# Layer-norm statistics partly on ScalarE, and the first two slabs of each up projection in buffers of their own

## The reference

```
for i in range(DEPTH):                                   # DEPTH = 2
    mix = _gmlp_mixer(h, ...) if i % 2 == 0 else _rwkv7_mixer(h, ...)
    h = _layer_norm(ALPHA * h + mix, ln1_g[i], ln1_b[i], LN_EPS)
    f = jnp.square(jax.nn.relu(h @ ffn_w1[i])) @ ffn_w2[i]
    h = _layer_norm(ALPHA * h + f, ln2_g[i], ln2_b[i], LN_EPS)

def _layer_norm(x, g, b, eps):
    mean = jnp.mean(x, axis=-1, keepdims=True)
    var = jnp.mean(jnp.square(x - mean), axis=-1, keepdims=True)
    return (x - mean) * lax.rsqrt(var + eps) * g + b
```

## Time and profile before

| | us |
|---|---|
| median of 3 runs | 1327.91 |
| lowest and highest | 1326.28, 1327.91 |
| the profiled execution's own time | 1330.27 |
| its span in the trace | 1328.6 |
| its mean granted TensorE clock | 0.988 of full speed |

### The profile page before, as it was taken

One profiled execution on the slowest core, in us unless ns is written; L12 is line 12 of the kernel. 1 busy time (PEld: TensorE's weight loads), 2 busy tenths in 40 slices (PEclk: granted clock), 3 DMA queues, 4 the chain that ended last, 5 costly groups with the idle time before them and its releaser, 6 DMA issues.

```text
span 1328.6 us, 22895 instructions
## 1 busy us (share of the span) xinstructions
PE 1282.6 (97%) x9137; PEld 1058.8 (80%) x9137; DVE 681.6 (51%) x922; ACT 497.3 (37%) x842; POOL 572.4 (43%) x353
## 2 busy tenths in 40 slices
PE   6999999999999998999999999999999999999996
PEld 5888788888888885487777888888798888888885
DVE  2486831112244468844478888876751111344447
ACT  4363232223223323234444667667222222322230
POOL 4344344444444452145454456644054444444440
PEclk9999999999999998999999999889999999999998
DMA  8234253332453331275443112112353333333321
GB/s 285 69 95 123 62 143 96 95 95 79 145 141 112 108 95 48 85 255 183 142 159 113 35 50 82 34 50 81 95 146 100 101 97 95 95 95 95 96 62 64
DMA packets 113579, 139.53 MB, mean 105 GB/s; under 512 B 10416, under 2 KB 86240, under 8 KB 113504
## 3 DMA queue, kind: packets, MB, share of 16 engines
q1 hardware_dynamic: 108896, 121.67, 30.5%
q10 hardware_dynamic: 4608, 16.78, 3.4%
HBM read 123.76 MB, written 14.68 MB: 104 GB/s over the span
## 4 chain that ended last, share of the span: by engine, by line
PE 76%; DVE 16%; ACT 4%; issue 2%; DMA 1%; SPq 1%; ACTq 0%; DVEq 0%
PE bank L1731 36%; PE bank L1826 9%; PE bank L1828 9%; PE bank L1827 9%; DVE a_lo L1181 2%; DVE gram L1539 2%; DVE x_tok L1211 2%; DVE x_tok L1213 2%; DVE stats L1200 2%; PE bank L1921 2%; DVE x_tok L1233 1%; PE bank L2038 1%; PE bank L2086 1%; PE bank L2204 1%; DMA raw<-in_gm_w_in 1%
## 5 line engine op out<-in xcount | busy, mean ns | idle before, releaser
L489 POOL TENSOR_TENSOR w_lo<-raw,w_hi 128x1024 fp32r<-128x1024 f32 x176 | 432.6, 2463 | 608.5 <-ACT w_hi L683 558.4
L683 ACT ACTIVATE w_hi<-raw 128x1024 fp32r<-128x1024 f32 x176 | 184.3, 1056 | 280.9 <-PE bank L1731 268.7
L1731 PE MATMUL bank<-w_hi,a_hi 128*128 128x512 f32 x756 | 234.8, 392 | 5.9 <-DVE a_lo L1181 5.9
L1826 PE MATMUL bank<-xT_hi,w_hi 128*128 128x512 f32 (+1 forms) x640 | 236.3, 369 | 3.9 <-POOL w_lo L489 3.9
L1827 PE MATMUL bank<-xT_lo,w_hi 128*128 128x512 f32 (+1 forms) x640 | 235.4, 368 | 0.0
L1828 PE MATMUL bank<-xT_hi,w_lo 128*128 128x512 f32 (+1 forms) x640 | 235.4, 368 | 0.0
L1731 PE MATMUL bank<-w_lo,a_hi 128*128 128x512 f32 x756 | 233.0, 389 | 0.0
L1731 PE MATMUL bank<-w_hi,a_lo 128*128 128x512 f32 x756 | 232.9, 389 | 0.0
L1181 DVE TENSOR_TENSOR a_lo<-big,a_hi 128x512 fp32r<-128x512 f32 x64 | 141.3, 2213 | 178.5 <-ACT a_hi L702 175.4
L1298 DVE TENSOR_TENSOR big<-relu 128x512 f32 (+1 forms) x64 | 45.8, 716 | 274.1 <-ACT relu L808 274.1
L1731 PEld LDWEIGHTS bank<-w_hi,a_hi 128*128 128x128 f32 x756 | 140.1, 188 | 40.4 <-issue 12.3
(11 more groups left out here) (310 smaller groups left out, 1639.6 us busy)
## 6 DMA issues: line engine op xcount, KB each, us to landing
raw<-in_ffn_w SPq DMA_DIRECT2D x128, 512.0 KB, 3.9
raw<-in_rw_w_rkv SPq DMA_DIRECT2D x24, 512.0 KB, 3.6
raw<-in_gm_w_in SPq DMA_DIRECT2D x16, 512.0 KB, 4.1
early<-proj SPq DMA_DIRECT2D x8, 1024.0 KB, 6.5
proj<-stage ACTq DMA_DIRECT2D x14, 512.0 KB, 3.6
proj<-low_stage ACTq DMA_DIRECT2D x10, 512.0 KB, 5.0
raw<-in_gm_w_out SPq DMA_DIRECT2D x8, 512.0 KB, 3.6
late<-proj SPq DMA_DIRECT2D x8, 512.0 KB, 4.1
```

Of the source, the lines that this page charges most:

```text
L489: nc.gpsimd.tensor_tensor(w_lo[:, j, :], raw[:, j, :], w_hi[:, j, :].bitcast(F32), ALU.subtract).then_inc(w_lo_ready, 1)
L683: nc.scalar.activation(w_hi[:, j, :], raw[:, j, :], ACT.Copy).then_inc(w_hi_ready, 1)
L1731: last = nc.tensor.matmul(bank[2 * t + h][:], a[:, j, tok], w[:, h * HALF:(h + 1) * HALF], start=start and m == 0, stop=stop and m == 2)
L1826: nc.tensor.matmul(dst, w_hi[:, j, col], xT_hi[:, k, tokens], start=k == 0, stop=False)
```

## The change

**Statistics.** For tiles 0 to 2 of each norm, `add` now also sums its output (`accum_out`). DVE forms the negative mean from the two sums (`less_mean`). ACT squares the whole tile with that as bias into a scrap buffer, with a sum (`square_sum`), and takes the root of it with scale 1/1024 and epsilon as bias (`deviation_of`). Tile 3 keeps `bn_stats`.

**Order on DVE.** The two passes over tile t - 1 now stand between the two `add`s of tile t, and for tile 2 further apart. `low_x` of tile 0 stands ahead of tile 3's first `add`, `low_x` of tile 1 behind its `bn_stats`.

**Own buffers.** The first two slabs of `up0` and `up1` are rounded into `first_hi` and their rest goes to `first_lo`, both in space of `big` that is idle then. So they wait for no slot of the row product; for `up1` they wait for the last readers of what lay there. Behind them ACT issues a root of epsilon, which loads the root's table.

```diff
+            def low_up(layer):
+                i = first_slab[f"up{layer}"] // SLOTS
+                for j in range(FIRST):
+                    pool.wait_ge(w_hi_ready, i * SLOTS + j + 1)
+                    nc.gpsimd.tensor_tensor(first_lo[:, j, :], raw[:, j, :], first_hi[:, j, :].bitcast(F32), ALU.subtract
+                                            ).then_inc(w_lo_ready, 1)
+                for j in range(FIRST, SLOTS):
+                    low_weights(i, j)
...
+            def deviation_of(norm, t):
+                count = (norm - 1) * (TT - 1) + t + 1
+                act.wait_ge(mean_ready, count)
+                nc.scalar.activation(junk[:], x_tok[:, t, :], ACT.Square, bias=less_mean[:, 0:1],
+                                     accum_out=square_sum[:]).then_inc(squares_summed, 1)
+                act.wait_ge(squares_summed, count)
+                nc.scalar.activation(std[:], square_sum[:], ACT.Sqrt, bias=eps[:, 0:1], scale=1.0 / D
+                                     ).then_inc(std_ready, 1)
...
             def finish_norm(name, count, norm, times, rounded=False):
+                if rounded:
+                    for j in range(FIRST):
+                        act.wait_ge(raw_in[j], 16 * ((first_slab[name] + count) // SLOTS + 1))
+                        if name == "rw_out":
+                            act.wait_ge(a_lo_ready, first_act[name] + KT)
+                            act.wait_ge(slab_used, first_slab[name] + SLOTS)
+                        nc.scalar.activation(first_hi[:, j, :], raw[:, j, :], ACT.Copy).then_inc(w_hi_ready, 1)
+                    nc.scalar.activation(std[:], eps[:], ACT.Sqrt)
+                deviation_of(norm, 0)
+                deviation_of(norm, 1)
+                if times is not None:
+                    turned(times, 0, rounded)
+                deviation_of(norm, 2)
+                if times is not None:
+                    turned(times, 1, rounded)
+                if rounded:
+                    for j in range(FIRST, SLOTS):
+                        round_weights(count // SLOTS, j, first_slab[name])
+                std_of(TT + norm)
...
+                for t in range(TT - 1):
+                    then(add(t, 0))
+                    if t:
+                        reciprocal_of(t - 1)
+                        centre(t - 1, whole, less_mean[:, 0:1], ALU.add)
+                        scaled(t - 1, whole).then_inc(x_ready, 1)
+                    then(add(t, 1))
+                    nc.vector.tensor_scalar(less_mean[:], y_sums[:, t % 2, 0:1], y_sums[:, t % 2, 1:2], -1.0 / D, ALU.add, ALU.mult
+                                            ).then_inc(mean_ready, 1)
...
+                def own(f):
+                    return (first_hi[:, f, :], first_lo[:, f, :]) if f < FIRST else None
                 for f in range(SLOTS):
-                    column_slab(0, f, n0, slice(0, 2 * P), False)
+                    column_slab(0, f, n0, slice(0, 2 * P), False, own(f))
```

More of the change, by code:

```diff
@@ L733, in turned, with std_of @@
                                          ).then_inc(xT_ready, 1)
-            def std_of(norm, t):
-                act.wait_ge(var_ready, norm * TT + t + 1)
+            def std_of(count):
+                act.wait_ge(var_ready, count)
                 nc.scalar.activation(std[:], mean_var[:, 1:2], ACT.Sqrt).then_inc(std_ready, 1)
-            def finish_norm(name, count, norm, times, rounded=False):
[L741 to L752, removed]
-                if times is not None:
-                    for t in range(2 if rounded else TT - 1, TT):
+            def deviation_of(norm, t):
[6 more added lines that the diff above has]
+                                     ).then_inc(std_ready, 1)
@@ L778, in _ @@
                 if f in (1, 2, 3, 4):
[L779 removed]
+                    std_of(f)
                 ahead(f // SLOTS, f % SLOTS, n0)
@@ L1204, in normalise @@
                                         ).then_inc(var_ready, 1)
-                if between is not None:
-                    between()
                 dve.wait_ge(std_ready, var_before + 1)
[L1208 to L1214, removed]
+                then(nc.vector.reciprocal(rstd[:, 0:1], std[:]))
+                then(nc.vector.scalar_tensor_tensor(y, y, mean_var[:, 0:1], gains[:, 0, :], ALU.subtract, ALU.mult))
+                nc.vector.scalar_tensor_tensor(y, y, rstd[:, 0:1], gains[:, 1, :], ALU.mult, ALU.add).then_inc(result, 1)
             def residual_norm(name, which, times, split=True):
@@ L1220, in residual_norm, with add @@
                 product = row_products.index(name)
[L1221 to L1229, removed]
-                        else:
[L1231 to L1240, removed]
+                def add(t, h):
+                    if h == 0:
+                        if t == 0:
+                            dve.wait_ge(tile_summed, product * (TT - 1) + 1)
+                        else:
+                            dve.wait_ge(half_summed, normed.index(name) * (TT - 1) + t)
+                    elif t < TT - 1:
+                        dve.wait_ge(tile_summed, product * (TT - 1) + t + 1)
+                    else:
+                        dve.wait_ge(slab_used, first_slab[name] + COUNT[name])
+                    y = x_tok[:, t, h * HALF:(h + 1) * HALF]
+                    return nc.vector.scalar_tensor_tensor(y, y, ALPHA, bank[2 * t + h][:], ALU.mult, ALU.add,
+                                                          accum_out=y_sums[:, t % 2, h:h + 1])
@@ new lines, in centre, with scaled, reciprocal_of @@
+                def centre(t, part, mean, op):
+                    y = x_tok[:, t, part]
+                    then(nc.vector.scalar_tensor_tensor(y, y, mean, gains[:, 0, part], op, ALU.mult))
+                def scaled(t, part):
+                    y = x_tok[:, t, part]
+                    return nc.vector.scalar_tensor_tensor(y, y, rstd[:, t % 2:t % 2 + 1], gains[:, 1, part], ALU.mult, ALU.add)
+                def reciprocal_of(t):
+                    dve.wait_ge(std_ready, (which + 1) * TT + t + 1)
+                    then(nc.vector.reciprocal(rstd[:, t % 2:t % 2 + 1], std[:]))
@@ new lines, in residual_norm @@
+                last = TT - 1
+                if times is not None and split:
+                    low_x(0, times)
+                then(add(last, 0))
+                done.inc(nc.vector.bn_stats(stats[:, 0, :], x_tok[:, last, parts[0]]))
+                if times is not None and split:
+                    low_x(1, times)
+                reciprocal_of(last - 1)
+                centre(last - 1, whole, less_mean[:, 0:1], ALU.add)
+                then(add(last, 1))
+                then(nc.vector.bn_stats(stats[:, 1, :], x_tok[:, last, parts[1]]))
@@ new lines, in residual_norm @@
+                then(nc.vector.bn_aggr(mean_var[:], stats[:].rearrange("p h s -> p (h s)")))
+                nc.vector.tensor_scalar(mean_var[:, 1:2], mean_var[:, 1:2], LN_EPS, None, ALU.add
+                                        ).then_inc(var_ready, 1)
+                scaled(last - 1, whole).then_inc(x_ready, 1)
+                reciprocal_of(last)
+                for part, ready in zip(parts, (x_half, x_ready)):
+                    centre(last, part, mean_var[:, 0:1], ALU.subtract)
+                    scaled(last, part).then_inc(ready, 1)
@@ L1268, in _ @@
                 split_x(t, 0)
+            then(nc.vector.memset(eps[:], LN_EPS))
             dve.wait_ge(gains_in, 32)
```

35 lines of the change are left out of this document (24 added, 11 removed).

## The result

The changed kernel took **1316.92 us** (median of 4 runs, 1316.32 to 1317.34), the kernel before 1327.5 beside it (4 runs): ratio 0.9921, 95% interval 0.9904 to 0.9939, 10.6 us faster. Both intervals leave out 1. The profiled execution took 1316.32 us, its span is 1314.5 and its granted clock 0.996.

What follows compares the result with a forecast made beforehand. TensorE, busy 97% of the span, bounds the kernel, so only its waits around the norms can pay: 2 x 3.1 (norms 1, 3) + 2 x 0.6 (norms 2, 4) = 7.4 us, from 1327.91 to 1320.5 us, range 1318.0 to 1325.5.

Steps and rivals of the forecast that it cites:

- Norm 4 is the same chain: Norm 4's tail behind TensorE's last matmul was taken to be like norm 2's, gaining 0.6 us.
- Up projections: First passes of up0 and up1: 3.44 us of stalls each, of which 3.1 us would be gained in each.
- The 0.3 us kept for `xT_lo`: First slab of an up projection: 0.3 of its 1.71 us wait remains, for xT_lo of tiles 0 and 1.
- the third stall: First pass of up0, turning of tile 3: TensorE waits 1.33 us, which the change would remove.
- Tiles 0 and 1, no gain: Statistics of tiles 0 and 1: x_ready comes where it was, since the saved instructions become waiting for TensorE; gain nothing.
- The sums: Writing out a sum with an add on DVE costs 0.1 us, and the same on ACT.
- Rival B: The sums are dear, at 0.7 us each: 6.0 us slower, 1333.9; decides from about 0.5 a sum; chance 0.07.
- the 0.5 us that ACT was to have to spare: Tile 0's root: ACT's sum hides behind TensorE's half tile with 0.5 us to spare, the root ready at about 142.8.
- The root's table, 0: Ahead of norm 1's first root: the 1.28 us table load is already finished early, so loading ahead is worth 0.
- Rival A: POOL starts ahead of DVE's pass over tile 2, margin 0.3 us: costs 1.3 us per up projection, time 1323.1; chance 0.17.
- Rival C: The stalls only move to the turnings, norms 2 and 4 give nothing: 2.8 us or less, 1325.1 and above; chance 0.11.
- The clock: Behind norm 2, TensorE's granted clock may shift the time by 1.5 us either way, in every case.

Runs made afterwards that it cites:

- s3_norm4_old: The changed kernel with the old code for norm 4 alone; 1319.73 us, norm 4 at 25.06.
- a1_after: The changed kernel again, nothing edited, on another chip; 1318.17 us, ratio 0.9935 to the kernel before.
- s1_buffers: The kernel before plus only the own buffers for the first two slabs of both up projections; 1324.97 us against 1326.74, ratio 0.9981.
- s2_stats: The changed kernel without the own buffers, so new order and statistics alone; 1323.34 us against 1326.74 for the kernel before, ratio 0.9975.
- s7_order_only: The changed kernel with bn_stats back on VectorE, no sums, ACT squares or root ahead; 1324.46 us against 1326.64 for the kernel before, ratio 0.9977.
- s4_no_root_ahead: The changed kernel without the root of epsilon that loads the root's table ahead; 1319.78 us.
- s5_pass_late: The changed kernel with tile 2's first pass behind the last add and its bn_stats in norms 1 and 3; 1322.81 us, ratio 0.9979 to the kernel before.

## Why the prediction was too low, step by step

**The step that failed** is "Norm 4 is the same chain" and the 0.6 us taken from it. Norm 2's tail behind PE was 7.03 us; norm 4's was 8.84, and I had not read it. After the change both have about the same tail, 6.31 in norm 4 and 518.11 - 511.83 = 6.28 in norm 2, since DVE no longer falls behind. PE's and DVE's timeline at the end of norm 2 after, for the earlier trace rows:

```profile
511.44 0.39 PE L1807 MATMUL bank<-w_hi,a_lo 128*128 128x512 f32 x1
```
```profile
517.36 0.75 DVE L1272 SCALAR_TENSOR_TENSOR x_tok<-x_tok,rstd,gains 128x512 f32<-128x512 f32 x1
```

Norm 2 gained 0.76, where 0.6 was forecast; norm 4 gained 2.55. s3_norm4_old shows it. With 2.55 in its place the same sum is 3.1 + 3.1 + 0.6 + 2.55 = 9.35, 1318.6. With all four as measured it is 10.3, and 1327.5 - 10.3 = 1317.2 is within 0.3 of the result. That the time came out at 1316.92 and not a little over 1318, as a1_after's 1318.17 did, goes with the granted clock (0.995 to 0.996 against mostly 0.993); that norm 4's gain was sized at a quarter does not depend on it.

**Up projections**: right mechanism, 3.5 in place of 3.1 each: all of the 3.44 us of stalls went. The 0.3 us kept for `xT_lo` came to nothing visible: the first slab's weight load has a wait of 0.39 in its row, but its first matmul starts right behind the product's last (157.70 + 0.39 = 158.09). s1_buffers and s2_stats show that the two parts need each other for the third stall.

**Tiles 0 and 1, no gain**: right against the kernel before, but s7_order_only shows that ACT's statistics are what holds this at nothing; without them norms 1 to 3 are 1.1 to 1.4 us longer each than in the changed kernel. The prediction costed the parts only together.

**The sums** (0.1 each): DVE's extra instruction takes 0.08 but lies in the end of the add: from an add to the next dependent instruction it is 0.72 us before (1301.05 to 1301.77) and 0.73 with the sum (159.42 to 160.15). ACT's takes 0.18. Rival B, which needed 0.5, is out. But the 0.5 us that ACT was to have to spare were 0.1 (143.31 to 143.43): the square, its sum and the root took until 143.31, not 142.8.

**The root's table, 0**: right in net. Its load is 1.28 us in the rows, and s4_no_root_ahead has 1.05 us of it on the path.
The Trainium skill ("ScalarE: Activation LUTs", section "What ACT_TABLE_LOAD costs") gives about 2.66 us for a change of table, 1.28 for the load and 1.38 for a drain. The trace agrees with the load, and a drain of that length does not show: in s4_no_root_ahead the load starts 0.01 us behind the square's sum and the root 0.02 behind the load.

**Rival A** did not come (158.10 against 158.64, so 0.5 us of margin, not 0.3), and s5_pass_late shows that it was a real one, 1.7 us each. **Rival C** is out: no stall moved.

**The clock**: I gave it 1.5 us behind norm 2 alone. Between two profiles of one kernel it made 3.75 us, most of it in the time mixing. So medians on two chips say 10.6 and 8.5 for a change whose columns give 10.3 us, and s1_buffers (1.8 measured, 4.6 in its columns) and s7_order_only (2.2 measured, 5.2 in its columns) look small. That the clock makes all of this is inferred from the middle column and the windows. In s1_buffers' runs, 1321.52 us goes with 0.993 and 1328.56 with 0.986. Why some versions are granted less clock than others stays open.

## What to carry to other kernels

Read the tail behind the last matmul at each place where a pattern recurs, and compare the period of each engine there: the same code was hidden under TensorE where TensorE also transposed (6.33 us a tile against VectorE's 6.15) and was the bound where it did not (5.44 against 6.15). Divide traces at marks before and behind each edit: sections repeat to 0.02 us where whole times vary by several us with the clock. Where two edits meet at one wait, cost each alone as well as both, for one may be what pays for the other.

## What the runs showed of the hardware

A sum on the side of an elementwise instruction is an instruction of its own: 0.08 us on VectorE, 0.18 on ScalarE. VectorE's adds from PSUM (0.69) and `bn_stats` (0.69) ran undisturbed beside GpSimd's subtraction, while a pass with SBUF operands alone was held up beside it (2.68 in place of 0.75). The load of ScalarE's table for the root took 1.28 us and ran ahead of a root that still waited for its input; with a square in between it came behind the square. TensorE's granted clock fell to its lower level (1.2 GHz, 0.50) behind norm 2 in every profile, for 3.4 to 10.2 us, also where transposes shortened TensorE's idle time there from 3.25 to 1.93 us, and elsewhere in some executions of a kernel and not in others.
